# The narrow h block's transposes of a MoE expert, one down piece later

## The reference, cut to what matters

```
def swiglu(x, wg, wu, wd):
    return (jax.nn.silu(x @ wg) * (x @ wu)) @ wd

def moe(xn, w_router, wg, wu, wd):
    ...
    top_vals, top_idx = lax.top_k(logits, TOP_K)       # 2 of 8 experts
    ...
    for e in range(N_EXPERTS):
        y = y + comb[:, e:e + 1].astype(t.dtype) * swiglu(t, wg[e], wu[e], wd[e])
```

## Time and profile before

| | us |
|---|---|
| runs: median of 3 (lowest to highest) | 1994.18 (1990.9 to 1994.24) |
| the profiled execution, its own time | 1993.76 |
| its span, first to last instruction | 1991.9 |
| PE busy in the span | 1953.0 (98%) |
| DVE, ACT busy | 1405.2 (71%), 1178.0 (59%) |
| the eight experts | from about 1200 to the end of the span |

### The profile page before, as it was taken

One profiled execution on the slowest core, in us unless ns is written; L12 is line 12 of the kernel. 1 busy time (PEld: TensorE's weight loads), 2 busy tenths in 40 slices (PEclk: granted clock), 3 DMA queues, 4 the chain that ended last, 5 costly groups with the idle time before them and its releaser, 6 DMA issues.

```text
span 1991.9 us, 27573 instructions
## 1 busy us (share of the span) xinstructions
PE 1953.0 (98%) x9292; PEld 1625.6 (82%) x9292; DVE 1405.2 (71%) x1665; ACT 1178.0 (59%) x1501; POOL 80.5 (4%) x104
## 2 busy tenths in 40 slices
PE   9989999999999999999998989999999999999998
PEld 7778888888888888888887878888888888888886
DVE  8766654644554454546666668989998989898996
ACT  7656544434434343435555657777777777777774
POOL 8200000000000000000200000000000000000000
PEclk9999999999999999999999999999999999999999
DMA  9544566566656656665654549999999999999996
GB/s 354 150 136 150 180 191 188 191 191 190 189 190 189 190 185 198 189 185 187 188 168 136 166 146 369 344 370 347 371 348 375 343 372 345 369 347 371 346 370 245
DMA packets 137235, 500.87 MB, mean 251 GB/s; under 512 B 15424, under 2 KB 15440, under 8 KB 135728
## 3 DMA queue, kind: packets, MB, share of 16 engines
q1 hardware_dynamic: 135440, 488.74, 71.7%
q0 software_dynamic: 1696, 10.86, 1.4%
HBM read 495.33 MB, written 4.20 MB: 251 GB/s over the span
## 4 chain that ended last, share of the span: by engine, by line
PE 87%; DMA 4%; DVE 3%; ACT 3%; POOL 2%; issue 2%; DVEq 0%; SPq 0%; ACTq 0%; POOLq 0%
PE main L546 27%; PE main L548 27%; PE main L547 27%; DMA raw_pieces<-in_ffn_moe 3%; DVE w_low L1297 1%; PE spread L889 1%; ACT w_high L972 1%; PE spread L890 1%; PE transpose L876 1%; PE transpose L915 1%; PE transpose L564 1%; PE transpose L745 0%; PE transpose L857 0%; DVE heads_scratch L1345 0%; DVE small L1346 0%
## 5 line engine op out<-in xcount | busy, mean ns | idle before, releaser
L1297 DVE TENSOR_TENSOR w_low<-raw_pieces,w_high 128x1024 fp32r<-128x1024 f32 x919 | 1095.1, 1221 | 419.4 <-ACT w_high L972 415.3
L972 ACT ACTIVATE w_high<-raw_pieces 128x1024 fp32r<-128x1024 f32 x919 | 941.9, 1058 | 248.6 <-DMA raw_pieces<-in_ffn_dense 124.5
L546 PE MATMUL main<-w_high,xT_high 128*128 128x512 f32 (+1 forms) x1920 | 734.8, 383 | 2.2 <-DVE w_low L1426 1.3
L548 PE MATMUL main<-w_high,xT_low 128*128 128x512 f32 (+1 forms) x1920 | 723.4, 377 | 0.0
L547 PE MATMUL main<-w_low,xT_high 128*128 128x512 f32 (+1 forms) x1920 | 722.5, 376 | 0.0
L546 PEld LDWEIGHTS main<-w_high,xT_high 128*128 128x128 f32 x1920 | 363.3, 189 | 67.0 <-issue 2.1
L548 PEld LDWEIGHTS main<-w_high,xT_low 128*128 128x128 f32 x1920 | 362.6, 189 | 66.9
L547 PEld LDWEIGHTS main<-w_low,xT_high 128*128 128x128 f32 x1920 | 363.3, 189 | 62.8
L546 PE MATMUL main<-w_high,hT_high 128*128 128x512 f32 x832 | 329.1, 396 | 0.0
L548 PE MATMUL main<-w_high,hT_low 128*128 128x512 f32 x832 | 324.6, 390 | 0.0
L547 PE MATMUL main<-w_low,hT_high 128*128 128x512 f32 x832 | 324.2, 390 | 0.0
(11 more groups left out here) (229 smaller groups left out, 954.7 us busy)
## 6 DMA issues: line engine op xcount, KB each, us to landing
raw_pieces<-in_ffn_moe SPq DMA_DIRECT2D x528, 512.0 KB, 5.3
raw_pieces<-in_ffn_dense SPq DMA_DIRECT2D x264, 512.0 KB, 3.6
raw_pieces<-in_w_in SPq DMA_DIRECT2D x96, 512.0 KB, 3.6
raw_pieces<-in_w_out SPq DMA_DIRECT2D x32, 512.0 KB, 3.6
x_resid<-in_x SPq DMA_DIRECT2D x4, 512.0 KB, 14.9
xn_rows<-token_major POOLq DMA_DIRECT2D x2, 1024.0 KB, 5.2
out_x<-x_resid SPq DMA_DIRECT2D x8, 256.0 KB, 2.6
token_major<-in_x_t SPq DMA_DIRECT2D x1, 1024.0 KB, 9.4
```

What stands on the lines that cost most here:

```text
L546: pe.matmul(out_ap, lh[ls], rh[rs], start=first, stop=False)
L548: return pe.matmul(out_ap, ll[ls], rh[rs], start=False, stop=last)
L972: act.activation(WH[:, piece % RING, :], RAWS[:, piece % RING, :], ACT.Copy).then_inc(high_done, 1)
L1297: dve.tensor_tensor(WL[:, piece % RING, :], RAWS[:, piece % RING, :], WH[:, piece % RING, :], ALU.subtract).then_inc(low_done, 1)
```

## The change

The transposes of block 5, the narrow one, move from behind position 37 to behind position 38: behind the third down piece instead of the second. ACT's copy moves with them from position 38 to 39 and DVE's remainder from 39 to 40. Position 41's wait stays where it was. The table is used for all eight experts (and a second pass over the experts that runs only if one expert has more than 128 tokens).

```
-E_TURN = {3: 0, 11: 1, 19: 2, 27: 3, 34: 4, 37: 5}
+E_TURN = {3: 0, 11: 1, 19: 2, 27: 3, 34: 4, 38: 5}
```

## The result

The changed kernel is slower: 1998.19 us median of 9 runs (1994.98 to 2000.7) against 1991.42 us (1987.23 to 1994.24) for the kernel before, a ratio of 1.0038 with a 95% interval of 1.0028 to 1.0047. That is 7.6 us, between 5.6 and 9.4; the two medians are 6.8 us apart. The prediction had 6.5 us, and 2000.3 us as the time.

What follows compares the result with a forecast made beforehand. PE was taken to set the time, with DVE and the weight stream almost without room. 7 x 0.80 + 0.90 = 6.5 us on 1993.76 gave 2000.3 us; forecast 1998.7 to 2002.2, range 1996.5 to 2003.0.

Steps and rivals of the forecast that it cites:

- The sum: Time PE loses before down piece 6 over eight experts: 7 x 0.80 + 0.90 = 6.5 us.
- the exchange of waits: PE waits about 1.4 us before down piece 6 where it waited 0.75 us before the narrow transpose.
- The wait removed: PE's wait for DVE's h block before the narrow transpose goes, some 5.6 us over eight experts.
- The wait added: PE waits before down piece 6 for DVE's remainder of chunk 10, about 1.2 us shown idle, 8 times.
- upper restart: PE starts down piece 6 0.13 us after DVE ends the remainder, the longer of 0.06 to 0.13 us.
- The fourth conversion: On DVE ahead of chunk 10's remainder: one more conversion of 1.13 us, running without waiting for ACT's rounding.
- The weight load: At down piece 6, the first matmul's weight load isn't covered behind the wait and adds 0.11 us.
- the rule on pulled loads: Skill page: PE pulls weight loads ahead of matmuls in flight; over down piece 6's wait this would save 0.9 us, giving 1999.4.
- (1): Rival: the gap before the transpose closes and no other wait replaces it; all 5.6 us won, 1988.1 us; chance 0.05.
- (2): Rival: DVE's fourth conversion is partly absorbed, down piece 6 starts when it did; 1993.8 us; chance 0.07.
- (3): Rival: the later start shrinks four other h-block waits, some 1.6 us, as the weight stream gets ahead; 1998.7 us; chance 0.10.
- (4): Rival: ACT's rounding is late, so DVE's fourth conversion waits too; half a microsecond per expert gives 2004.3 us; chance 0.05.

Runs made afterwards that it cites:

- third experiment: Against the changed kernel, ACT's copy and DVE's remainder both moved to position 38, PE's transposes left behind 38; 0.9971 of the kernel before, median 1984.88 us.
- all at 39: Against the kernel before, block 5's transposes moved behind position 39 and ACT's copy to 39, DVE's remainder left at 39; 0.9986 of its time.
- products swapped: Transposes, copy and remainder at 39, 40, 41, against the kernel before, and down piece 6's product not reading chunk 10 put first; 1.0072, 14.3 us above.
- two positions later: Against the kernel before, block 5's transposes, copy and remainder moved from 37, 38, 39 to 39, 40, 41; 1.0134, 26.7 us above.

## Why the prediction was right

**The number.** The increase was 6.5 us in the forecast, and 6.8 by the medians or 7.6 by the ratio. The time, 1998.19 us, lies in the wide range (1996.5 to 2003.0) but just below the forecast's own band of 1998.7 to 2002.2. The sum was added to the one profiled execution of 1993.76 us, and the median of nine runs of the kernel before is 1991.42, 2.3 us lower. The start of the sum was off, not the exchange of waits.

**What bounds the kernel.** PE's time was the time, and a wait that ended on DVE was the place to look. The third experiment says the same from the other side: without both waits the kernel is 5.8 us faster.

**The wait removed.** Predicted 5.6 us and the transpose 0.23 us behind its predecessor; seen so in all eight experts of the changed kernel.

**The wait added.** Predicted: remainder 1.13 us later, restart 0.06 to 0.13 us behind DVE's end, a first matmul of 0.33 instead of 0.22 us, about 1.2 us of shown idle. Seen: 1.15 us later; 1261.03 to 1261.16, which is the upper of the two restarts; 1261.16 to 1261.49, 0.33 us; idle 1.31. PE waits 1.47 us by starts, where I had 1.4. With the upper restart my sum had 0.83 per expert and 6.8 us in all (7 x 0.83 + 0.96), inside the measured 5.6 to 9.4. By the sum's own terms the eighth expert is 0.93 in the middle and the width 6.2 to 6.8, where the prediction wrote 0.90 and 6.1 to 6.7. The upper restart came in seven experts; in the eighth PE started 0.06 us behind DVE's end (1961.26 to 1961.32).

**The fourth conversion runs without waiting.** It hung on a margin of 0.01 to 0.14 us at ACT. The merged row of four conversions, 4.62 us long, has no gap in it, and ACT's copy was done long before.

**The weight load.** The uncovered load of 0.11 us is there: 0.33 instead of 0.22 us between the first two matmuls. The row that I took it from was the wrong one, though, and the number was right by luck: the 0.33 us of the earlier trace rows stand behind a transpose, and in the changed kernel, where the transpose waits for nothing, the distance there is 0.32 us all the same (1256.85 to 1257.17). PE's weight-load row in the eighth expert of the changed kernel starts with its matmul and not ahead of the wait, as in the other seven, to within 0.01 us:

```profile
1961.32 0.19 PEld L546 LDWEIGHTS main<-w_high,hT_high 128*128 128x128 f32 x1 [1.58 <-DVE hT_low L1680]
1961.32 0.50 PE L546 MATMUL main<-w_high,hT_high 128*128 128x512 f32 x1 [1.15 <-DVE hT_low L1680]
```

By this a load is not pulled over a semaphore wait, and the 0.9 us that the sum would have lost by the rule on pulled loads are not lost.

**The rivals.** (1), the gap closes: true only if DVE's remainder is moved the other way, which is the third experiment. (2), the even exchange: no conversion was absorbed, see the 1.15 us. (3), other waits shrink: in the profiled execution they did, from four with about 1.6 us to two with 0.5 us, more than I had in the forecast. From the first h block's transposes to the last matmul the profiled executions differ by 783.2 - 777.8 = 5.4 us, and not by the some 6.9 us exchanged at the narrow block (by starts 12.6 us added, 5.7 taken away). Whether that is the later start or chance stays open: the kernel with only the remainder later, whose down piece 6 is as late, shows three such waits, one of them of 1.5 us, and the one with all at 39 has two, of 0.3 and 0.2. Over the ten traces, one for each kernel, these waits come to between 0.3 and 2.0 us, and not in the order of the delay. (4) did not occur.

**A side remark that was too easy.** I wrote that the clock would not fall in the longer wait, because it had not in 0.9 us. That was right for 1.3 us; the two kernels with longer waits show that it was right by about half a microsecond, since the clock fell behind 1.78 and 1.81 us.

## What to carry to other kernels

Here PE makes the transposed chunk and later reads it back, and DVE, which works in a fixed order, stands in between. Taking PE off one wait didn't help as long as DVE's step for the next wait moved back with it. So look up the slack of the next wait (0.54 us here) before shifting its supplier by a step that is longer (1.13 us). The position of a step on the engine that produces a result and its position on the engines that copy it out can be chosen separately: the same move of the transposes was worth 7.6 us more or 5.8 us less, by where copy and remainder stood. And an idle gap on TensorE may cost more than its length: here it did behind some of the gaps of 1.8 us and more, and behind none of 1.3 us.

## What the runs showed of the hardware that I had not expected

TensorE's clock fell to its lower level behind idle times of 1.8 us in two experts (fourth and seventh, products swapped), and stayed at its higher one behind 2.54 us in another (fourth, two positions later). With 1.3 us of idle, in the changed kernel, it fell in no expert; with 1.7 to 2.0 us it fell behind two waits of eight, with 2.4 to 2.7 us behind six of eight. Each fall cost 1.3 to 1.6 us where I worked it out, about as much as the whole wait of the changed kernel. So one more conversion of 1.13 us per expert raised the loss from 7.6 to 26.7 us, of which some 9 us are the clock's.
